# Moving the memory keys and values of a fused two-block kernel from the attention loop to the first stage

## The reference, cut to what matters

```python
# first block
mod = silu(c) @ w_mod + b_mod                    # (1024) @ (1024, 6144), for c and for c_ctx
hx = modulate(rmsnorm(x, norm1_g), sh1, sc1)     # sh1, sc1: columns 0..2047 of mod
hc = modulate(rmsnorm(ctx, norm1_g), csh1, csc1)
p, pc = hx @ w_in, hc @ w_in                     # queries, keys, values
x = x + g1 * (attention(p, pc) @ w_out)
x = x + g2 * moe(modulate(rmsnorm(x, norm2_g), sh2, sc2))   # 32 experts, 4 for each token
x = rmsnorm(x, final_g)
# second block
kv_me = rmsnorm(mem, norm_mem) @ w_mem_kv        # (256, 1024) @ (1024, 1024): needs nothing of x
k_me, v_me = kv_me[:, :512], kv_me[:, 512:]
o_me = memory_attention(q_me, k_me, v_me)        # beside two other kinds of attention
...
```

## Time and profile before

| | |
|---|---|
| median of 3 runs | 1724.51 us (1720.22 to 1726.79) |
| profiled execution, time | 1721.17 us |
| profiled execution, span | 1719.4 us |
| mean granted TensorE clock | 0.983 of full |
| PE busy | 92% of the span |
| ahead of the experts (0 to 289 us) | 17% of the span |
| experts (289 to 1223 us) | 54% |
| second block (1223 to 1719 us) | 29% |

### The profile page before, as it was taken

How to read it: one execution, slowest core, us unless ns; L and a number is a source line. 1 busy time by engine, 2 the same in 40 slices (tenths; PEclk the granted TensorE clock), 3 DMA queues, 4 the chain that set the end, 5 groups by cost and what they waited for, 6 DMA issues and landing times.

```text
span 1719.4 us, 23854 instructions
## 1 busy us (share of the span) xinstructions
PE 1589.9 (92%) x10048; PEld 995.7 (58%) x10048; DVE 545.0 (32%) x1092; ACT 444.1 (26%) x856; POOL 7.3 (0%) x16
## 2 busy tenths in 40 slices
PE   4999899999999999999999999999699989899997
PEld 3786676434443444343334434443399978889997
DVE  3754513101010101011110101010355564478763
ACT  3434623101010100001010101010445542355642
POOL 0000000000000000000000000000000100000000
PEclk9999998999999999999999999999899989999999
DMA  9325853999999999999999999999634523425420
GB/s 394 149 96 204 337 164 117 433 419 425 423 435 431 433 430 431 432 430 434 431 432 431 431 430 431 431 433 430 271 119 152 184 99 130 164 99 194 166 107 25
DMA packets 27429, 524.75 MB, mean 305 GB/s; under 512 B 2931, under 2 KB 7027, under 8 KB 7492
## 3 DMA queue, kind: packets, MB, share of 16 engines
q1 hardware_dynamic: 24368, 519.06, 72.8%
q10 hardware_dynamic: 2484, 3.19, 0.7%
q0 software_dynamic: 512, 1.57, 0.4%
HBM read 522.72 MB, written 1.08 MB: 305 GB/s over the span
## 4 chain that ended last, share of the span: by engine, by line
PE 86%; DVE 6%; ACT 4%; issue 2%; DMA 1%; ACTq 0%; DVEq 0%; SPq 0%
PE ps L577 83%; PE ps L904 1%; ACT arena L1325 1%; ACT arena L1341 1%; DMA ring<-in_first 1%; DMA arena<-in_ctxT 1%; DVE arena L1788 1%; DVE arena L1781 1%; DVE arena L1785 1%; DVE mx L1637 1%; ACT arena L1256 0%; PE ps L1015 0%; DVE arena L1539 0%; PE ps L893 0%; PE ps L705 0%
## 5 line engine op out<-in xcount | busy, mean ns | idle before, releaser
L577 PE MATMUL ps<-ring,arena 128*64 128x512 f32 (+1 forms) x3872 | 709.6, 530 | 25.8 <-ACT arena L1341 24.4
L577 PEld LDWEIGHTS ps<-ring,arena 128*64 128x64 f32 (+1 forms) x3872 | 251.2, 132 | 457.2 <-issue 454.5
L577 PE MATMUL ps<-arena_r,w_high 128*128 128x256 f32 x1840 | 340.3, 288 | 10.2 <-DVE arena_r L1840 9.4
L577 PEld LDWEIGHTS ps<-arena_r,w_high 128*128 128x128 f32 x1840 | 290.7, 194 | 15.4 <-issue 12.7
L577 PE MATMUL ps<-arena 64*128 64x256 f32 (+7 forms) x1812 | 267.0, 379 | 15.6 <-ACT arena L1325 11.7
L577 PE MATMUL ps<-arena_r,ring_r 128*128 128x256 f32 x920 | 262.7, 286 | 0.0
L1779 DVE TENSOR_SCALAR arena<-ps 128x512 f32<-128x512 f32 x32 | 22.2, 692 | 749.0 <-PE ps L577 749.0
L577 PEld LDWEIGHTS ps<-arena 64*128 64x128 f32 (+4 forms) x1812 | 173.1, 178 | 99.0 <-issue 74.2
L577 PEld LDWEIGHTS ps<-arena_r,ring_r 128*128 128x128 f32 x920 | 178.7, 194 | 0.0
L1814 DVE TENSOR_TENSOR ring_r<-ring,w_high 128x1024 fp32r<-128x1024 f32 x120 | 142.0, 1221 | 85.4 <-ACT w_high L1362 85.4
L1334 ACT ACTIVATE arena<-arena 128x512 f32<-128x512 f32 x32 | 20.1, 630 | 499.4 <-DVE arena L1779 499.4
(11 more groups left out here) (205 smaller groups left out, 1012.8 us busy)
## 6 DMA issues: line engine op xcount, KB each, us to landing
ring<-in_w_gate_up SPq DMA_DIRECT2D x64, 4096.0 KB, 17.9
ring<-in_w_down SPq DMA_DIRECT2D x32, 4096.0 KB, 15.0
ring<-in_second SPq DMA_DIRECT2D x32, 2048.0 KB, 8.1
ring<-in_first SPq DMA_DIRECT2D x19, 2048.0 KB, 9.6
ring<-in_first SPq DMA_DIRECT2D x3, 1024.0 KB, 4.8
ring<-in_second SPq DMA_DIRECT2D x2, 1024.0 KB, 5.0
small<-in_small ACTq DMA_DIRECT2D x1, 1024.5 KB, 8.5
arena<-in_xT SPq DMA_DIRECT2D x1, 1024.0 KB, 8.3
```

Source lines behind the costliest of these rows:

```text
L577: return nc.tensor.matmul(out_, lhsT, rhs, start=start, stop=stop, **kw)
```

## The change

The memory's keys and values are computed in the first stage.

- SP loads `memT` ahead of `xT`, and the whole of the keys' weights (2 MiB in one load) into slot 4 of the ring behind the context. In the stream the values' weights stand between the third and the fourth unit of `w_mod`. `w_in` now follows from unit 5 on. The two loads of half the keys' weights are gone. The bytes are the same in sum.
- ACT squares the memory first, then `xT` and the context. The sigmoid of `c` keeps its place behind the latter.
- DVE's program keeps its start (with the wait on `csig_set`); behind it now stand the reciprocal and the eight products of the memory, and then those of `xT` and the context.
- PE's program is: squares of the memory (bank 7), squares of `xT` and the context (bank 6), memory jobs 0 and 1 (keys), modulation rounds 0 to 2, memory job 2, round 3, memory job 3, `project(0)`.
- ACT copies the four results to a buffer `k_me1`, `v_me1`; its program has the copy of job 3 ahead of the high parts 1 to 3 of `w_in`. POOL (GpSimd) copies them to the old place at the end of the attention loop, and the second block waits for that.
- DVE modulates chunks 0 to 3 behind round 2, and chunks 4 to 7 behind round 3.
- In the attention loop modulation rounds 4 to 11 move from steps 8 to 15 to steps 5 to 12. Steps 13 to 15 have no filler.
- The fourth memory job ahead of the router is gone, and ACT's copy of it.

```diff
@@ stream
-FIRST = [blocks("w_mod", 512 * u, 512) for u in range(4)]
+KEYS = blocks("w_mem_kv_2", 0, 512)
+FIRST = [blocks("w_mod", 512 * u, 512) for u in range(3)]
+U_KV = len(FIRST)
+FIRST += [blocks("w_mem_kv_2", 512, 512), blocks("w_mod", 512 * 3, 512)]
 U_IN = len(FIRST)
 FIRST += [blocks("w_in", 512 * u, 512) for u in range(4)] + [blocks("w_in", 2048, 256)]
-U_KV = len(FIRST)
-FIRST += [blocks("w_mem_kv_2", 0, 256), blocks("w_mem_kv_2", 512, 512)]
...
-        freed = [(ada_mm, n + 1) for n in range(4)]
+        freed = [(ada_mm, n + 1) for n in range(3)] + [(kv_mm, 4), (ada_mm, 4)]
...
@@ SP
+            sp.dma_start(memT, io["memT"]).then_inc(mem_in, 16)
             sp.dma_start(xT, io["xT"]).then_inc(x_in, 16)
             sp.dma_start(hx[:, :, T:2 * T], io["ctxT"]).then_inc(ctx_in, 16)
+            sp.dma_start(ring[:, SLOT_KEYS, :], keys).then_inc(slot_full[SLOT_KEYS], 16)
...
@@ POOL
+            pool.wait_ge(proj_mm, len(JOBS))
+            pool.wait_ge(kv_act, 4)
+            nc.gpsimd.tensor_copy(k_me, k_me1).then_inc(kv_moved, 1)
+            nc.gpsimd.tensor_copy(v_me, v_me1).then_inc(kv_moved, 1)
...
@@ PE
-            sum_squares(NORM1, sq, 7, 2 * T)
+            sum_squares(NORM_MEM, sq_m, 7, T)
+            sum_squares(NORM1, sq, 6, 2 * T)
...
+            def memory_job(n):
+                kind, i = KV_JOBS[n]
+                at = SLOT_KEYS if kind == "k" else U_KV % RING1
+                w = slot(at, KC)
+                if n == 0:
+                    pe.wait_ge(mem_set, KC)
+                if n >= 2:
+                    pe.wait_ge(kv_act, n - 1)
+                pe.wait_ge(slot_full[at], 16)
...
+            memory_job(0)
+            memory_job(1)
             pe.wait_ge(cs_set, 1)
-            for n in range(4):
+            for n in range(3):
                 ada_rows(n, 5)
                 ada_turn(n, COL_BANKS[n])
+            memory_job(2)
+            ada_rows(3, 5)
+            ada_turn(3, COL_BANKS[3])
+            memory_job(3)
...
-                if MEM_JOB < n <= MEM_JOB + 4:
-                    k = 2 * (n - MEM_JOB - 1)
-                    pe.wait_ge(brow_set, 2)
-                    sum_squares(NORM_MEM, sq_m, 7, T, k, k + 2)
...
-                if kv_at(a) is not None:
-                    memory_job(kv_at(a))
...
             sum_squares(NORM2, sq2, 2, T)
-            memory_job(3)
...
@@ ACT
+            act.wait_ge(mem_in, 16)
+            for k in range(KC):
+                square(NORM_MEM, k, sq_m[:, k % 2], memT[:, k])
+            root(NORM_MEM, 7)
             act.wait_ge(x_in, 16)
             act.wait_ge(ctx_in, 16)
             for k in range(KC):
...
             act.wait_ge(small_in, 16)
             A(csig[:], col("cvec"), ACT.Sigmoid).then_inc(csig_set, 1)
             load_table(ACT.Sqrt)
...
-            for n in range(4):
+            copy_memory(0)
+            copy_memory(1)
+            for n in range(3):
                 ada_copy(n, 5)
...
+            for k in range(KC // 2):
+                normed_hi(k)
+            copy_memory(2)
+            ada_copy(3, 5)
+            split_hi1(0)
+            for k in range(KC // 2, KC):
+                normed_hi(k)
+            copy_memory(3)
             for p in range(1, HI_PARTS):
                 split_hi1(p)
...
@@ DVE
-            dve.wait_ge(root_set, 1)
+            inverse_rms(NORM_MEM)
+            for k in range(KC):
+                times(memT[:, k], memT[:, k], col("mem_g")[:, k:k + 1]).then_inc(mem_set, 1)
+
+            dve.wait_ge(root_set, NORM1 + 1)
             link(V.reciprocal(r1, rope1))
...
+            for n in range(3):
+                ada_columns(n, COL_BANKS[n])
+            scales(0)
+            for half in range(2):
+                for k in range(KC // 2):
+                    modulated(k, half)
+            for k in range(KC // 2):
+                normed_lo(k, 0)
+            ada_columns(3, COL_BANKS[3])
+            scales(1)
+            for k in range(KC // 2, KC):
                 modulated(k, 0)
             split_lo1(0)
-            for k in range(KC):
+            for k in range(KC // 2, KC):
                 normed_lo(k, 0)
...
             split_lo1(1)
-            for k in range(KC):
+            for k in range(KC // 2, KC):
                 modulated(k, 1)
```

More of the change, by code:

```diff
@@ L53 @@
 SLOT_C = (4, 2, 3, 0, 1)
+SLOT_KEYS = 4
 PART = 1024
@@ L112 @@
 FIRST += [blocks("w_out", 512 * u, 512) for u in range(2)]
-U_KV2 = len(FIRST)
-FIRST += [blocks("w_mem_kv_2", 256, 256)]
 U_MOE = len(FIRST)
+U_MOD = (0, 1, 2, U_KV + 1) + tuple(range(U_MOD2, U_OUT))
 V_IN = 0
@@ L328, in build @@
         w_gu, w_dn = io["w_gate_up"], io["w_down"]
-        first, second = units("first", FIRST), units("second", SECOND)
+        (keys, *first), second = units("first", [KEYS, *FIRST]), units("second", SECOND)
         def unit_dst(index, src):
@@ L484, in build @@
         block = ctx.enter_context(nc.Block())
-        freed = [(ada_mm, n + 1) for n in range(4)]
+        freed = [(ada_mm, n + 1) for n in range(3)] + [(kv_mm, 4), (ada_mm, 4)]
         freed += [(proj_mm, 1 + max(LAST_JOB[p] for p in range(N_PARTS1) if PARTS1[p][0] == U_IN + u)) for u in range(5)]
-        freed += [(kv_mm, 1), (kv_mm, 3)]
-        freed += [(ada_mm, n + 1) for n in range(4, 12)] + [(out_mm, 2), (out_mm, 4), (kv_mm, 4)]
+        freed += [(ada_mm, n + 1) for n in range(4, 12)] + [(out_mm, 2), (out_mm, 4)]
         freed_c = [(br_mm, 4 * (c - V_BR) + 4) if V_BR <= c < V_OUT
@@ L1215, in _ @@
                     act.dma_start(bias_rows.ap().rearrange("(g h) n -> h g n", g=2), brow[0:8]).then_inc(bias_out, 16)
-                if MEM_JOB <= n < MEM_JOB + 4:
-                    act.wait_ge(mem_in, 16)
-                    for k in range(2 * (n - MEM_JOB), 2 * (n - MEM_JOB) + 2):
-                        square(NORM_MEM, k, sq_m[:, k % 2], memT[:, k])
-                if n == MEM_JOB + 4:
-                    root(NORM_MEM, 7)
             act.wait_ge(lam_set, 1)
@@ L1522, in _ @@
             neg_lam = lamv[:, 1:2]
-            dve.wait_ge(root_set, 1)
-            link(V.reciprocal(r1, rope1))
-            for k in range(KC):
-                V.tensor_tensor(hx[:, k, 0:T], xT[:, k], r1[:, 0:T], ALU.mult)
-                last = V.tensor_tensor(hx[:, k, T:2 * T], hx[:, k, T:2 * T], r1[:, T:2 * T], ALU.mult)
-            link(last)
             rinv = nrm[:, 0]
@@ L1539, in times @@
                 return V.scalar_tensor_tensor(dst, src, g, rinv, ALU.mult, ALU.mult)
+            inverse_rms(NORM_MEM)
+            for k in range(KC):
+                times(memT[:, k], memT[:, k], col("mem_g")[:, k:k + 1]).then_inc(mem_set, 1)
+            dve.wait_ge(root_set, NORM1 + 1)
+            link(V.reciprocal(r1, rope1))
+            for k in range(KC):
+                V.tensor_tensor(hx[:, k, 0:T], xT[:, k], r1[:, 0:T], ALU.mult)
+                last = V.tensor_tensor(hx[:, k, T:2 * T], hx[:, k, T:2 * T], r1[:, T:2 * T], ALU.mult)
+            link(last)
             def ada_columns(n, bank):
@@ L1622, in _ @@
                 rope(n)
-                if n == MEM_JOB + 4:
-                    inverse_rms(NORM_MEM)
-                    for k in range(KC):
-                        times(memT[:, k], memT[:, k], col("mem_g")[:, k:k + 1]).then_inc(mem_set, 1)
             def maxima(a):
@@ L2071 @@
     weights["w_ffn_up_2"] = x["w_ffn_up_2"].reshape(D, 2, FC // 2, 2 * P).transpose(0, 2, 1, 3).reshape(D, -1)
-    arrays["first"], arrays["second"] = laid_out(FIRST, weights), laid_out(SECOND, weights)
+    arrays["first"], arrays["second"] = laid_out([KEYS, *FIRST], weights), laid_out(SECOND, weights)
     arrays["b_gate_up"], arrays["b_down"] = x["b_gate_up"], x["b_down"]
```

102 lines of the change are left out of this document (41 added, 61 removed).

## The result

The kernel with the change takes 1735.60 us in the median (1734.12 to 1737.08, 5 runs), the one before 1723.07 (1720.22 to 1726.79, 5 runs). The ratio is 1.0074, with a 95% interval from 1.0061 to 1.0087: slower by 10.5 to 15.0 us. The forecast was 1739 in the range 1730 to 1747. The profiled execution has a span of 1733.6, 14.2 more than before; the sum of the forecast was 16.1.

What follows compares the result with a forecast made beforehand. PE's chain was taken to bound the kernel (86%). The terms +28.2 - 3.5 - 7.6 - 1.0 = +16.1 us put the profiled execution at 1737.3 and the median at 1740.6; the forecast was 1739, range 1730 to 1747.

Steps and rivals of the forecast that it cites:

- the first term: First stage, up to projection job 2: its start moves from 57.22 to 85.4, +28.2 us, bounds +22 and +31.
- Steps 1 and 2: First stage, squares: the memory's from 9.9 take 6.5 us; with those of xT and context PE is through at 25.2.
- Step 3: First stage, memory's norm: DVE has the sigmoid ahead of it; memory job 0 starts at 31.2, PE idle 6.0 us.
- Rival A: First stage: the memory's norm isn't held back, job 0 at 25.3 with a warm clock; +7.7 us, 1730; chance 6%.
- Step 4: First stage, memory jobs 0 and 1: 7.1 us each plus 2.4 for a halved clock, done at 47.8.
- Step 5: First stage, rounds 0 to 2 at 2.6 us each, then job 2, round 3 and job 3, done at 72.2.
- Step 6: From project(0) at 72.2 to projection job 2 at 85.4: DVE sets the pace, ACT held on job 3's copy.
- Squares in the projections: Four groups of two sums of squares leave PE's chain there: -3.5 us, bounds -4.1 and -3.
- Attention: Attention loop: steps 5 to 7 give back 6.8 of 21.4 us, steps 13 to 15 0.8; -7.6, bounds -4 and -22.
- Rival C: Attention loop: PE is its bound, so all 21.4 us of the jobs come back; +2 us, 1725; chance 4%.
- Router: Ahead of the router's logits: the fourth memory job is gone, -1.0 us, between 0 and -2.2.
- Rival D: A new wait, for w_in's third unit freed by job 3, or another clock fall between rounds; +21 us, 1744; chance 12%.

Runs made afterwards that it cites:

- Experiment 1: Changed kernel with the memory's reciprocal and eight products ahead of DVE's wait for the sigmoid; 1727.69 us, ratio 1.0036 to the kernel before.
- experiment 2: Changed kernel with six more matmuls of 512 columns on PE between the squares and memory job 0; 1737.75 us, ratio 1.0090 to the kernel before.
- experiment 4: Changed kernel with each of the four memory jobs summing one chunk of eight (wrong keys and values); 1717.64 us, ratio 0.9973 to the kernel before.
- experiment 3: Changed kernel with ACT's copy of memory job 3 behind the high parts 1 to 3; 1737.19 us, ratio 1.0097 to the kernel before.
- Experiment 5: Kernel before with the memory jobs of attention steps 5 to 7 summing one chunk of eight (wrong keys and values); 1715.21 us, ratio 0.9955.
- router_warm: Changed kernel with four filler matmuls of 512 columns on PE ahead of the router's logits; 1733.58 us, ratio 1.0085 to the kernel before.
- Experiment 6: Kernel before with only the fourth memory job, ahead of the router's logits, summing one chunk of eight; 1722.79 us, ratio 1.0000.
- split_warm: Keys' jobs at the start, values' jobs in attention steps 5 and 6, norm first, late copy, four fillers ahead of the logits; 1725.08 us, 1.0015 to the kernel before.

## Why the prediction was right

The direction and the mechanism are confirmed, and the size within 2 us. That the sum came so near is in part luck: up to the experts the first term was 2.9 us too large, the router's 1.7 too small, and the two partly cancelled. Its steps, one by one:

- **Steps 1 and 2**, squares. Forecast and measured: first matmul 9.9 and 8.94, since `memT` landed a little earlier than `small` had; memory's squares 6.5 and 6.09 us; PE through with the others at 25.2 and 24.0. All is some 1 us early.
- **Step 3**, DVE held by the sigmoid: job 0 at 31.2 and 29.64, behind a pause of 6.0 and 5.63 us. Experiment 1 shows that it is DVE's order and nothing else. The Trainium skill, "TensorE: Matmul & The Clock Gate", section "Architectural detail: the array is 16× 32×32, not 1× 128×128", has ACT and DVE take instructions strictly first in, first out; DVE's wait of 15.16 us with a ready root behind it agrees. Rival A has fallen.
- **Step 4**, the jobs: 16.6 forecast, 15.6 measured. The clock cost 1.6 to 1.7 us and not 2.4 (experiments 1 and 2).
- **Step 5**, rounds and jobs 2 and 3: 7.8 and 7.7 us for three rounds, `project(0)` at 72.2 and 68.9. The stream stayed hidden; experiment 4 has its floor at 52.7.
- **Step 6**, from `project(0)` to projection job 2: 13.2 and 13.6, with ACT held on the copy as foreseen, which experiment 3 prices at 1.5. The first term, +28.2, is +25.3: this is the term that was mis-sized, by three small excesses, 1.6 us ahead of job 0, 1.0 in jobs 0 and 1, and 0.7 from there to `project(0)`; step 6 took 0.4 more than forecast. It lay within its bounds.
- **Squares in the projections:** -3.5 forecast, -3.4 measured (from +25.3 to +21.9).
- **Attention:** -7.6 forecast, -8.0 measured, of which 7.2 in steps 5 to 7 (6.8 was forecast) and 0.8 behind. The sum on DVE in step 5 (L1694) came 9.7 us behind step 4's maxima, 9.8 was forecast. Experiment 5 gave 7.1 with the jobs at their old place cut down. Rival C has fallen.
- **Router:** -1.0 forecast, +0.7 measured, outside its bounds of 0 and -2.2. From the output projection to the logits nothing changed (+0.05): that is the bound of 0, which the forecast gave for a falling clock (a pause of 3.41 us, then 0.50). The other bound, -2.2 at full clock, is near what `router_warm` showed (-2.0). The middle of the two was a price for neither. Behind the logits, up to the experts, 0.7 us was lost, for which there was no term; `router_warm` doesn't lose it (its clock was full until 282), which points to the clock but doesn't show it. Experiment 6 shows that PE's part of the fourth job was free.
- **POOL's copies:** 0, as forecast. **Rival D**, a new wait, didn't occur: the unit of `w_in` was split by ACT ahead of job 3's end, and PE went from job 3 to `project(0)` without a pause.
- **Expert stage:** there was no term for it. It became 1.4 us shorter (from the experts' first matmuls to the last expert's, 926.4 and 925.0), and the second block 1.0 us longer. The eight profiles of the kernel after and of those derived from it have 924.1 to 925.0 us here, the three of the kernel before and of experiments 5 and 6 have 926.4 each, so this isn't chance. One wait became shorter, PE's for a copy of ACT in each expert (L1341 before, L1346 after): 24.4 us in 32 before, 22.0 in 32 after. Why it did wasn't tested and stays open.

The median went up by 12.5 us and the profiled span by 14.2. The profile of before (1721.17) lies 1.9 below the median of its runs, and a clock that falls at another place moved a profile by 1.5 us (experiments 2 and 3), so the two figures don't contradict each other. The forecast's sum of 16.1 lies just above the interval of 10.5 to 15.0. In the time of the whole kernel, 1739 lay 3.4 above 1735.60: the sum put the profiled execution at 1737.3, 1.7 too high, and the other 1.7 were added because the median of the kernel before lay above its profile. In the kernel after the profiled execution is itself the median.

## What to carry to other kernels

Price a moved step at both ends. Where it was, ask for what the engine would have waited without it; here 28 us of PE's work cost some 7, as the chain through DVE and ACT set the step's length. Where it goes, follow each of its inputs along the queue of the engine that makes it; nine instructions behind a wait for something else were about half of the loss, the fallen clock behind it included. And ask whether the engine that makes an early input waits, ahead of it in its program, for something that the input doesn't need.

## What the runs showed of the hardware

- **A clock that stays down while PE is busy.** In the kernel after PE stood 3.41 us ahead of the logits. The clock was full until 274, 0.81 at 274 to 276 us and 0.50 from there:

```profile
274.00:276.00 2.00, 0.00 (x0) 0.00 (x0) 1.81 (x2) 1.61 (x3) 0.00 (x0) 0.81 1.23 528
...
278.00:280.00 2.00, 2.00 (x11) 2.00 (x11) 1.20 (x4) 1.77 (x5) 0.00 (x0) 0.50 0.83 360
280.00:282.00 2.00, 2.00 (x12) 2.00 (x11) 0.00 (x0) 0.00 (x0) 0.00 (x0) 0.50 1.21 512
```

  PE was fully busy with small matmuls (32 columns) from 278 on, and the clock stayed at half through all of it. The Trainium skill, "TensorE: Matmul & The Clock Gate", section "HAM oscillation — how this bites in real kernels", has a TensorE that waits between short bursts of matmuls run the next burst at half clock. There the wait is for loads. These rows agree for a wait on ACT and DVE, and so does the pause of 5.63 us ahead of job 0, which stands behind 7.80 us of squares (0.50 at 28 to 29 us). That the clock stays down through busy matmuls is told by these rows alone.
- **A free filler has a use.** The fourth memory job covered PE's wait and kept the clock up through the logits: 3.65 us with it, 7.03 and 6.96 without (the kernel after and experiment 6). It therefore neither cost nor saved anything. Four filler matmuls in its place did so in `router_warm` and not in `split_warm` (4.99 and 6.21 us). Whoever takes idle-time work off PE should look at what the clock takes back; here it was all of the 2.2 us.
- **The place of a fall isn't fixed.** With the same program around it and the same pause of 1.83 us ahead of it, the round near 166 us ran at full clock in the kernel after (1.95 us) and at half in experiments 2 and 3 (3.62 and 3.40), in one profile each. Changes worth 1.5 us upstream, real in their own stretch, didn't reach the end.
